# Half of the blocks under HGRN's levels multiplied whole in float32, the others in parts with the remainder on VectorE

## The reference

```python
proj = jnp.einsum('bld,dc->blc', xn, w_in)
q, zf_fwd, zf_bwd, inp, og, hy, gates = jnp.split(proj, IN_SPLITS, axis=-1)
...
logf = jnp.log(lbh + (1.0 - lbh) * jax.nn.sigmoid(zh))
k = (1.0 - lbh) * jax.nn.sigmoid(-zh)
...
b = jnp.cumsum(fb, axis=2)
diff = b[:, :, :, None, :] - b[:, :, None, :, :]
decay = jnp.exp(jnp.where(incl, diff, -jnp.inf))
scores = jnp.einsum('nhtk,nhsk,nhtsk->nhts', qb, kb, decay)
intra = jnp.einsum('nhts,nhsv->nhtv', scores, vb)
```

## Time and profile before

| | |
|---|---|
| median of 3 runs | 2725.11 us (2724.31 to 2730.82) |
| the profiled execution | 2729.77 us, span 2728.0 us |
| granted clock of TensorE, mean | 0.942 of full speed |
| busy: PE, DVE, ACT, POOL | 90%, 66%, 43%, 32% |
| the stage of the change | 1333.7 to 1573.1 us |

### The profile page before, as it was taken

The page is one execution under the profiler, slowest core; times in us unless marked ns, Lnnn a source line. Parts: engine busy times, 40 slices in busy tenths (PEclk is TensorE's granted clock), DMA queues, the critical chain, the costliest instruction groups (busy, mean ns, idle before and its releaser), DMA issues.

```text
span 2728.0 us, 39068 instructions
## 1 busy us (share of the span) xinstructions
PE 2461.4 (90%) x16062; PEld 2228.1 (82%) x16062; DVE 1812.3 (66%) x2717; ACT 1183.5 (43%) x1915; POOL 879.8 (32%) x404
## 2 busy tenths in 40 slices
PE   6968888999999999997767978798999999999997
PEld 5856678999999788886757966598999999888885
DVE  4565446978888555556597266365997888555554
ACT  3333234444444444443544254234444444444442
POOL 3000002886666000001154544100886666100000
PEclk8878889999999999998888888899999999999998
DMA  5412234554444566663422333134555444566663
GB/s 164 132 55 70 86 94 146 164 170 147 147 146 145 177 190 187 188 189 113 128 85 78 116 117 122 57 108 162 168 168 159 145 145 148 168 187 189 187 188 105
DMA packets 108568, 384.40 MB, mean 141 GB/s; under 512 B 13007, under 2 KB 16000, under 8 KB 107816
## 3 DMA queue, kind: packets, MB, share of 16 engines
q1 hardware_dynamic: 108392, 381.91, 45.0%
HBM read 380.79 MB, written 1.06 MB: 140 GB/s over the span
## 4 chain that ended last, share of the span: by engine, by line
PE 75%; DVE 16%; ACT 3%; POOL 3%; issue 1%; DMA 1%; SPq 0%; DVEq 0%; POOLq 0%; ACTq 0%
PE psum L349 21%; PE psum L350 21%; PE psum L351 21%; PE psum L1757 4%; POOL weight_parts L328 2%; PE psum L511 1%; PE psum L2374 1%; PE psum L2147 1%; ACT weight_parts L317 1%; DVE peer_experts L1665 1%; PE psum L1222 1%; DVE weight_parts L322 1%; DVE peer_experts L1664 1%; DVE peer_experts L1641 1%; DVE peer_experts L1633 1%
## 5 line engine op out<-in xcount | busy, mean ns | idle before, releaser
L349 PE MATMUL psum<-acts_high,weight_parts 128*128 128x256 f32 x3296 | 972.8, 295 | 65.4 <-DVE acts_low L543 28.4
L328 POOL TENSOR_TENSOR weight_parts<-weight_ring,weight_parts 128x1024 fp32r<-128x1024 f32 x314 | 808.0, 2582 | 554.2 <-ACT weight_parts L317 553.6
L350 PE MATMUL psum<-acts_low,weight_parts 128*128 128x256 f32 x3296 | 944.7, 287 | 0.0
L351 PE MATMUL psum<-acts_high,weight_parts 128*128 128x256 f32 x3296 | 944.4, 287 | 0.0
L317 ACT ACTIVATE weight_parts<-weight_ring 128x1024 fp32r<-128x1024 f32 x702 | 736.8, 1050 | 161.3 <-PE psum L351 138.9
L349 PEld LDWEIGHTS psum<-acts_high,weight_parts 128*128 128x128 f32 x3296 | 643.9, 195 | 82.4 <-issue 42.5
L322 DVE TENSOR_TENSOR weight_parts<-weight_ring,weight_parts 128x1024 fp32r<-128x1024 f32 x388 | 477.4, 1232 | 319.9 <-ACT weight_parts L317 319.8
L350 PEld LDWEIGHTS psum<-acts_low,weight_parts 128*128 128x128 f32 x3296 | 645.4, 196 | 2.5 <-issue 1.7
L351 PEld LDWEIGHTS psum<-acts_high,weight_parts 128*128 128x128 f32 x3296 | 644.1, 195 | 0.0
L349 PE MATMUL psum<-weight_parts,peer_coef 128*128 128x512 f32 x1024 | 406.6, 397 | 4.0 <-issue 3.9
L350 PE MATMUL psum<-weight_parts,peer_coef 128*128 128x512 f32 x1024 | 406.3, 397 | 0.0
(11 more groups left out here) (380 smaller groups left out, 2451.4 us busy)
## 6 DMA issues: line engine op xcount, KB each, us to landing
weight_ring<-in_peer_down SPq DMA_DIRECT2D x128, 512.0 KB, 3.6
weight_ring<-in_peer_up SPq DMA_DIRECT2D x128, 512.0 KB, 3.6
weight_ring<-in_peer_u SPq DMA_DIRECT2D x128, 512.0 KB, 3.5
weight_ring<-in_peer_v SPq DMA_DIRECT2D x128, 512.0 KB, 4.2
weight_ring<-in_w_in SPq DMA_DIRECT2D x88, 512.0 KB, 3.7
weight_ring<-in_w_out SPq DMA_DIRECT2D x16, 512.0 KB, 3.5
weight_ring<-in_peer_w_q SPq DMA_DIRECT2D x16, 512.0 KB, 3.6
weight_ring<-in_w_in_v SPq DMA_DIRECT2D x10, 512.0 KB, 3.5
```

Of the source, the lines that this page charges most:

```text
L328: q.e.tensor_tensor(self.low, self.ring, self.high.bitcast(F32), ALU.subtract).then_inc(*self.unit.ready.once())
L349: q.e.matmul(out, sh, mh, start=first, stop=False)
L350: q.e.matmul(out, sh, ml, start=False, stop=False)
L351: return q.e.matmul(out, sl, mh, start=False, stop=last)
```

## The change

Before the two blocks w[0] and w[1] are fetched, `c.whole` is set, and from then on every other submission of the 40 blocks sets it anew: 21 blocks are fetched whole (18 of channels, 3 of tokens), 19 are split, now with the remainder on VectorE. A whole block isn't split: TensorE multiplies it in float32 straight from the ring, with the input in `work`, 8 matmuls of 128x256 (or 4 of 128x512), and its place in the ring is free when they are done. Since `work` is now read by these blocks, and the heads write there, the rest of the 40 blocks is planned ahead of the heads (`finish`), and so are the two splits for the next stage, which go back to GpSimd.

```diff
+class Whole(Step):
+    def __init__(self, c, src):
+        self.src, self.unit = src, Unit()
+        slot = c.loaded % c.SLOTS
+        c.loaded += 1
+        self.ring, self.slot_free = c.ring[:, slot, :], c.slot_free[slot]
+        self.unit.whole, self.unit.slot, self.unit.ready = self.ring, slot, c.landed[slot].next()
+    def sync(self, q):
+        q.wait_ge(self.slot_free)
+        q.e.dma_start(self.ring, self.src).then_inc(*self.unit.ready.once())
...
+    def fetch(self, src):
+        return self.plan(Whole(self, src) if self.whole else Split(self, src)).unit
...
+        else:
+            self.weights = unit.whole.rearrange("p (k c) -> p k c", k=KD)
+            c.slot_free[unit.slot] = acts.whole_free = self.done
...
+                last = q.e.matmul(self.out, w[:, k, :], acts.whole[:, k, :], start=k == 0, stop=k == KD - 1)
...
+                    last = q.e.matmul(whole.out[i], acts.whole[:, k, tile], w[:, kk, :], start=k == 0,
+                                      stop=k == KD - 1)
...
     def scalar(self, q):
-        q.wait_ge(self.mixed)
+        q.wait_ge(self.mixed, self.o_free)
...
+    o_free = finish()
     for hd in range(HG_H):
-        c.hg_taken = c.plan(HgrnHead(c, s, hd, v, o)).taken
+        c.hg_taken = c.plan(HgrnHead(c, s, hd, v, o, o_free)).taken
...
+            c.whole = True
             c.flush(w[0], w[1])
             projected = c.last_kept
             c.rotation = [4, 5, 6]
-            c.low_by = "pool"
...
-            filler = more()
-            together(hgrn(c, inner, s, q, zf, zb, projected, v, o), filler, 1)
-            for _ in filler:
-                pass
-            c.flush(w[32], w[40])
+            def in_turns(units):
+                for n, _ in enumerate(units):
+                    c.whole = n % 2 == 0
+                    yield
+            filler = in_turns(more())
+            def finish():
+                for _ in filler:
+                    pass
+                c.whole = False
+                c.low_by = "pool"
+                c.flush(w[32], w[40])
+                return xn.whole_free
+            together(hgrn(c, inner, s, q, zf, zb, projected, v, o, finish), filler, 1)
...
+        xn.whole = work
```

More of the change, by code:

```diff
@@ L187, with __init__ @@
 class Parts:
-    def __init__(self, high, low):
+    def __init__(self, high, low, whole=None):
         self.high, self.low, self.marks, self.free = high, low, [None] * KD, None
+        self.whole, self.whole_free = whole, None
 class Core:
@@ L212, in __init__ @@
         self.low_by = "vector"
+        self.whole = False
         self.jobs, self.prepared = [], []
@@ L362, in __init__ @@
         self.marks = list(acts.marks)
-        self.done = c.part_free[unit.part] = acts.free = c.mark("multiplied")
+        self.done = c.mark("multiplied")
+        if unit.whole is None:
+            self.weights = c.parts[:, unit.part, :, :].rearrange("p x (k c) -> p x k c", k=KD)
+            c.part_free[unit.part] = acts.free = self.done
+        else:
+            self.weights = unit.whole.rearrange("p (k c) -> p k c", k=KD)
+            c.slot_free[unit.slot] = acts.whole_free = self.done
         c.last_product = self.done
@@ L371, in tensor @@
             q.wait_ge(self.marks[k])
-            last = product(q, self.out, (w[:, 0, k, :], w[:, 1, k, :]), (acts.high[:, k, :], acts.low[:, k, :]),
-                           k == 0, k == KD - 1)
+            if self.unit.whole is None:
+                last = product(q, self.out, (w[:, 0, k, :], w[:, 1, k, :]), (acts.high[:, k, :], acts.low[:, k, :]),
+                               k == 0, k == KD - 1)
+            else:
+                last = q.e.matmul(self.out, w[:, k, :], acts.whole[:, k, :], start=k == 0, stop=k == KD - 1)
         last.then_inc(*self.done.once())
@@ L396, in __init__ @@
         self.whole, self.unit, self.n = whole, unit, n
-        self.weights = c.parts[:, unit.part, :, :].rearrange("p x (k c) -> p x k c", k=whole.n_k)
         if n == 0:
@@ L402, in __init__ @@
         self.marks = list(whole.acts.marks)
-        self.done = c.part_free[unit.part] = whole.acts.free = c.mark("multiplied")
+        self.done = c.mark("multiplied")
+        if unit.whole is None:
+            self.weights = c.parts[:, unit.part, :, :].rearrange("p x (k c) -> p x k c", k=whole.n_k)
+            c.part_free[unit.part] = whole.acts.free = self.done
+        else:
+            self.weights = unit.whole.rearrange("p (k c) -> p k c", k=whole.n_k)
+            c.slot_free[unit.slot] = whole.acts.whole_free = self.done
         c.last_product = self.done
@@ L420, in tensor @@
                 q.wait_ge(self.marks[k])
-                last = product(q, whole.out[i], (acts.high[:, k, tile], acts.low[:, k, tile]),
-                               (w[:, 0, kk, :], w[:, 1, kk, :]), k == 0, k == KD - 1)
+                if self.unit.whole is None:
+                    last = product(q, whole.out[i], (acts.high[:, k, tile], acts.low[:, k, tile]),
+                                   (w[:, 0, kk, :], w[:, 1, kk, :]), k == 0, k == KD - 1)
+                else:
+                    last = q.e.matmul(whole.out[i], acts.whole[:, k, tile], w[:, kk, :], start=k == 0,
+                                      stop=k == KD - 1)
         last.then_inc(*self.done.once())
```

13 lines of the change are left out of this document (7 added, 6 removed).

## The result

The changed kernel takes 2706.91 us (median of 4 runs, 2702.18 to 2707.74), the kernel before 2724.71 us beside it (4 runs, 2721.95 to 2730.82). The ratio is 0.9933, with a 95% interval of 0.9916 to 0.9951: the change makes the kernel faster, by about 18 us. Forecast were 2712 us, with a range of 2704 to 2725.

The account below looks back on a forecast made before the run. The prediction took VectorE's chain up to the last scaling, then TensorE's backlog, to bound the stage. Gain 18.7 - 2.6 = 16.1 us, less 3 us, gives 13 us: from the median 2725.1 to 2712 us, range 2704 to 2725.

Parts of the forecast that it names:

- the backlog: TensorE's work from the fourth pair's last scaling to the stage's last block: 61.4 us before, 64.0 us forecast.
- GpSimd silent: In this stage 38 remainders leave GpSimd, so VectorE's instructions are no longer stretched: 36.5 us off VectorE.
- the walk: VectorE's chain followed through the stage's four pairs of levels: last scaling at 1491.7 instead of 1510.4, gain 18.7 us.
- The subtractions: VectorE gets 19 in the stage, 1.23 us each, 23.4 us; 12 stand ahead of the last scaling, 15 us.
- The new wait: A split block's load waits for the whole block three before it; subtraction done 6.1 to 6.9 us after that block's end.
- A whole block: On TensorE 3.45 us against 2.88 in parts; 21 add 12.0 us, before 1510 in TensorE's idle time.
- four passes: Rival: a whole block takes TensorE 3.84 us, eight in the backlog cost 3.1 us more, 2715 us; chance 0.03.
- The roundings: 21 of 1.05 us leave ScalarE, which waits for TensorE where it sets the pace; counted as nothing.
- Heads last: The eight heads come behind all blocks instead of between them: 7.2 us in both orders, no difference.
- late subtractions and changes of kind: In the backlog: up to 0.3 us a pair, and 10 to 15 product changes at 0.1 us; together 3 us.
- longer waits: Rival: VectorE's three waits behind whole blocks each grow 3.4 us at low clock, leaving 2723 us; chance 0.24.
- slower by turns: Rival: four more subtractions ahead of the last scaling wait 5.8 us, VectorE and TensorE alternate, 2735 us; chance 0.06.

Follow-up runs that it names:

- experiment 1: The changed kernel, with GpSimd doing an unused subtraction into a spare buffer beside each of the 19 subtractions: 2721.96 us, ratio 0.9984 to the kernel before.
- experiment 4: The changed kernel with all 40 blocks whole, so no subtraction in the stage: 2704.15 us, ratio 0.9913 to the kernel before.
- experiment 2: The changed kernel with no block whole, all 40 in parts and all remainders on VectorE: 2718.41 us, ratio 0.9973 to the kernel before.
- experiment 8: The changed kernel with the first 24 submissions whole, the rest in parts, and a ring of four places: 2693.41 us, ratio 0.9878 to the kernel before.
- experiment 5: The kernel before, with only the heads and the stage's ending steps planned behind all 40 blocks: 2726.34 us, ratio 1.0002.
- experiment 3: The changed kernel with the 19 remainders on GpSimd instead of VectorE: 2718.95 us, ratio 0.9967 to the kernel before.
- experiment 7: The changed kernel with a ring of four places instead of three: 2696.01 us, ratio 0.9881 to the kernel before.
- experiment 6: The changed kernel with the first 24 submissions whole and the rest in parts, ring of three: 2705.67 us, ratio 0.9923 to the kernel before.

## Why the prediction was right, and by how much it was off

The direction and the mechanism held: faster, by VectorE's stretch going and by waits behind whole blocks taking part of it back. The time came out 5 us lower than forecast. Two terms of the backlog were wrong and offset each other, which was luck. By the steps:

1. **GpSimd silent: 36.5 us off VectorE.** Right. (The 2.0 us of one more stretched instruction, ahead of the scans, were in the walk and not in this sum.) Every scan takes 0.66 to 0.69 us and no 128x1024 tensor_tensor is above 1.23. The dummy brings 14 us of time back (experiment 1).
2. **The subtractions.** Right: 1.22 us each, and 12 ahead of the last scaling, as counted.
3. **The new wait.** The chain of its parts was right to 0.2 us. The first was to come behind a whole block; that block ends near 1359.15, the next load is issued at 1359.19, and the subtraction is done at 1365.11, 5.96 us later (predicted 6.1). The three waits were 3.68, 0.42 and 6.51 us, forecast about 6, 1 and 7. The first was mis-sized, and this is half of the 5 us. VectorE's timeline has all three:

```profile
1363.88 1.23 DVE L343 TENSOR_TENSOR weight_parts<-weight_ring,weight_parts 128x1024 fp32r<-128x1024 f32 x1 [3.68 <-ACT weight_parts L338]
...
1409.00 1.23 DVE L343 TENSOR_TENSOR weight_parts<-weight_ring,weight_parts 128x1024 fp32r<-128x1024 f32 x1 [0.42 <-ACT weight_parts L338]
...
1463.43 1.23 DVE L343 TENSOR_TENSOR weight_parts<-weight_ring,weight_parts 128x1024 fp32r<-128x1024 f32 x1 [6.51 <-ACT weight_parts L338]
```

   I had let the first block after TensorE's idle time run at low clock from end to end. It ran at low clock from 1351.18 only up to some 1354.3 and took 4.4 us in place of 5.8 (twice 2.88): two rows of the table of stretches of the changed kernel show the clock.

```profile
1351.00:1355.50 4.50, 4.32 (x24) 4.32 (x25) 3.66 (x7) 2.15 (x3) 0.00 (x0) 0.63 0.41 120
1355.50:1365.00 9.50, 9.50 (x57) 8.71 (x56) 5.82 (x10) 2.10 (x4) 0.00 (x0) 1.00 0.34 110
```

   My walk put the first pair at 52.0 us from the keys and the last at 150.9; they came at 49.7 and 148.4. The 2.3 us of the first pair went through nearly unchanged (the masks of the second and third pair came 2.4 and 2.3 us ahead of the walk), so nothing else in the walk cancelled. The clock is 1.4 of them; where the other 0.9 arose, the record doesn't show.
4. **A whole block.** Right: 3.46 us against 3.45, and 6.33 us for a pair of blocks, which is 3.45 + 2.88, so that a change between the two kinds of product costs nothing that the trace can show; the 0.1 us that the sum put on each stood on no row. The Trainium skill, FP8 and Floating Point Precision, TensorE Precision Notes, gives true FP32 four passes. The 3.84 us that the prediction made of this prices a pass like a one-pass product at full clock, 0.12 us, and that reading is refuted, but the four passes are not. At low clock the one-pass products of the changed kernel recur every 0.213 us (ten in a row from 1351.99 to 1354.12) and the exact ones every 0.86, four for one. At full clock they recur every 0.12 and 0.43 us, 3.6 for one: the one-pass products gain less by the doubled clock. Why, no run here shows. What the step had wrong is that ahead of the last scaling this lies in TensorE's idle time. It didn't matter for the total here, but it is part of why experiment 4 missed by 12 us.
5. **The roundings.** Nothing gained by their going was the forecast; no run takes them away alone, so it stands untested. That ScalarE's list also holds exponentials and roundings behind the copies of results was in the walk only at two places; experiments 2, 4 and 8 show it as a cause of its own.
6. **Heads last.** Right: 0 (experiment 5). They recur every 0.89 us, and the last one's copy is followed at once by the next stage's table, in ScalarE's timeline (to be laid beside the earlier trace rows):

```profile
1551.39 0.39 ACT L2213 ACTIVATE work<-psum 128x256 f32<-128x256 f32 x1 [0.51 <-PE psum L2209]
1552.29 0.38 ACT L2213 ACTIVATE work<-psum 128x256 f32<-128x256 f32 x1 [0.51 <-PE psum L2209]
1552.92 1.28 ACT L2264 ACT_TABLE_LOAD   x1 [0.25 <-ACTq L626]
```

   Before, the stage's last block was kept 11.5 us ahead of the next stage's first instruction on VectorE; now the last head is 10.9 us ahead. These 0.5 us, from the remainders that no longer end the stage, I had set at nothing.

The backlog was forecast at 64.0 us and up to 3 more. TensorE's row of the first products of the last pair (to be laid beside the earlier trace rows) and the last head give 1486.51 to 1552.29, 65.8 us:

```profile
1486.51 2.88 PE L2185 MATMUL psum<-hg_q,hg_k 128*128 128x128 f32 x16 [2.45 <-issue]
1489.18 4.47 PE L402 MATMUL psum<-work,weight_ring 128*128 128x256 f32 x16
```

The sum had let the start at low clock (1.9 us) go. It stayed: the clock from 1486.5 to 1490.0 was 0.64, the first products recur after 2.67 us where the next do after 1.79, and the whole block behind them after 4.30 instead of 3.46, 1.7 us together. The 3 us for late subtractions and changes of kind were not needed: TensorE was busy for 59.49 of the 59.60 us up to 1546.00. So 64.0 + 3 was 1.2 us too much, by two errors that nearly cancel.

The miss is then 2.3 (first wait) + 0.2 (rest of the walk) + 1.2 (backlog) + 0.5 (end), 4.2 us against the 4.5 by which the stage's gain of 17.5 exceeds my 13.

Of the rivals, "longer waits" and "slower by turns" rested on the waits adding to the chain in full. Experiments 3 and 7 show that they needn't: with the 10.6 us gone, VectorE waited for scores instead, and with 6.6 of them gone, 2.7 came through. Most came through where a wait stood ahead of a pair's differences, as in experiment 6: VectorE's idle time grew by 5.9 us (32.9 to 38.8) for 8.7 us of waits.

## What to carry to other kernels

Before giving an idle engine a share of the work, look at what it does to the others' durations: work of 2.4 us on GpSimd cost VectorE some 2.15 us wherever it kept VectorE out, more than the 1.22 us of doing it itself, and the loss showed as slow VectorE work. Where engines hand over to each other, a wait that is removed can come back, in part or in full, under another name; add up an engine's idle time over the walk, not the one wait. And where more than one version has a side effect on the whole program (here a fourth place in the ring), run that alone in the kernel before.

## What the runs showed of the hardware beyond this

- VectorE and GpSimd exclude each other by whole instructions, in both directions: before, a remainder that takes 2.36 us alone was recorded with 8.19 us behind a row of VectorE's work. Mask copies out of PSUM weren't kept out: before, one of 1.32 us at 1478.44 lay wholly within a remainder of 2.38 us, neither of them longer than alone.
- An exact float32 product of 128x256 takes 0.43 us at full clock, three one-pass products 0.36 (2.88 / 8): 1.2 times the price. At low clock it is 0.86 against 0.64 (3 x 0.213), 4 / 3.
- Runs of one kernel spread over 3 to 13 us here (the changed one with four places 2690.83 to 2701.92, 11 us), and their mean granted clocks with them: 0.954 in the fastest, 0.950 in the slowest. A single profile can stand 5 us off its median, which is why the stage's milestones were the better witness.
